# Key and probability transposes of a latent attention moved from TensorE to DMA, and five joins moved to GpSimd

## The reference, cut to what matters

```python
q = (_rmsnorm(q_lat, q_norm_g) @ wq_b).reshape(b, s, MLA_HEADS, MLA_NOPE + MLA_ROPE)
kv = (_rmsnorm(kv_lat, kv_norm_g) @ wkv_b).reshape(b, s, MLA_HEADS, MLA_NOPE + MLA_V)
k_nope, v = kv[..., :MLA_NOPE], kv[..., MLA_NOPE:]
k = jnp.concatenate([k_nope, jnp.broadcast_to(k_pe[:, :, None, :], (b, s, MLA_HEADS, MLA_ROPE))], axis=-1)
q = _rmsnorm(q, qn_g)
k = _rmsnorm(k, kn_g)
...
    sc = jnp.einsum('bhqd,bhkd->bhqk', q_blk, k).astype(jnp.float32) * scale
    p = jax.nn.softmax(sc, axis=-1)
    return jnp.einsum('bhqk,bhkd->bhqd', p, v)
...
return jax.nn.silu(gate) * o
```

## Time and profile before

| what | value |
|---|---|
| time, median of 3 runs (lowest, highest) | 787.43 us (787.29, 787.88) |
| the profiled execution: its time, its span | 787.68 us, 785.9 us |
| PE busy | 778.7 us, 99% of the span |
| DVE, ACT, POOL busy | 558.9, 414.9, 31.6 us |
| DMA | 163.02 MB, mean 207 GB/s |
| time from the issue of a 512 KB load to its landing | median 4.3 us |

### The profile page before, as it was taken

The page is one execution under the profiler, slowest core; times in us unless marked ns, Lnnn a source line. Parts: engine busy times, 40 slices in busy tenths (PEclk is TensorE's granted clock), DMA queues, the critical chain, the costliest instruction groups (busy, mean ns, idle before and its releaser), DMA issues.

```text
span 785.9 us, 9964 instructions
## 1 busy us (share of the span) xinstructions
PE 778.7 (99%) x3852; PEld 659.2 (84%) x3852; DVE 558.9 (71%) x712; ACT 414.9 (53%) x579; POOL 31.6 (4%) x36
## 2 busy tenths in 40 slices
PE   8999999999999999999999999999999999999998
PEld 7988878888888888888889888788888888888887
DVE  5873599678576756767896727997785697566684
ACT  7686756545444634533564676565555364454331
POOL 0111110000000000000000201100000000000000
PEclk9999999999999999999999999999999999999999
DMA  8895774686564837868867857765684648478875
GB/s 294 274 329 189 255 227 158 167 216 211 186 180 141 243 108 213 237 185 251 233 194 238 272 173 237 206 197 169 171 252 149 188 148 237 128 196 244 202 233 165
DMA packets 97086, 163.02 MB, mean 207 GB/s; under 512 B 57856, under 2 KB 60416, under 8 KB 96912
## 3 DMA queue, kind: packets, MB, share of 16 engines
q1 hardware_dynamic: 96432, 159.93, 68.5%
q10 hardware_dynamic: 432, 1.22, 0.5%
q0 software_dynamic: 176, 1.25, 0.4%
HBM read 147.17 MB, written 2.10 MB: 190 GB/s over the span
## 4 chain that ended last, share of the span: by engine, by line
PE 85%; DVE 10%; ACT 2%; issue 1%; POOL 1%; DMA 1%; SPq 0%; ACTq 0%
PE pair L525 56%; PE bank L484 14%; PE pair L484 6%; DVE lo L1097 4%; PE bank L452 1%; ACT work L989 1%; PE bank L445 1%; PE bank L567 1%; PE bank L768 1%; PE bank L662 1%; PE bank L758 1%; DVE yT L1349 1%; ACT hi L805 1%; POOL work L1652 1%; DMA raw<-stream 1%
## 5 line engine op out<-in xcount | busy, mean ns | idle before, releaser
L1097 DVE TENSOR_TENSOR lo<-raw,hi 128x1024 fp32r<-128x1024 f32 (+3 forms) x264 | 307.0, 1176 | 127.3 <-ACT hi L805 125.2
L805 ACT ACTIVATE hi<-raw 128x1024 fp32r<-128x1024 f32 (+3 forms) x264 | 264.1, 1021 | 208.5 <-PE pair L525 77.8
L525 PE MATMUL pair<-hi,xT_hi 128*128 128x512 f32 (+1 forms) x768 | 205.8, 388 | 2.3 <-ACT hi L805 1.2
L525 PE MATMUL pair<-lo,xT_hi 128*128 128x512 f32 (+1 forms) x768 | 202.6, 384 | 0.7 <-DVE lo L1097 0.7
L525 PE MATMUL pair<-hi,xT_lo 128*128 128x512 f32 (+1 forms) x768 | 202.7, 384 | 0.0
L525 PEld LDWEIGHTS pair<-lo,xT_hi 128*128 128x128 f32 x768 | 142.7, 188 | 29.0 <-DVE lo L1097 1.5
L525 PEld LDWEIGHTS pair<-hi,xT_lo 128*128 128x128 f32 x768 | 142.9, 188 | 28.1
L525 PEld LDWEIGHTS pair<-hi,xT_hi 128*128 128x128 f32 x768 | 140.3, 188 | 30.1 <-issue 2.0
L484 PE MATMUL bank<-hi,yT 128*128 128x512 f32 x320 | 79.0, 389 | 0.0
L484 PEld LDWEIGHTS bank<-hi,yT 128*128 128x128 f32 x320 | 60.1, 188 | 12.5
L484 PE MATMUL bank<-lo,yT 128*128 128x512 f32 x160 | 42.8, 389 | 0.0
(11 more groups left out here) (174 smaller groups left out, 638.6 us busy)
## 6 DMA issues: line engine op xcount, KB each, us to landing
raw<-stream SPq DMA_DIRECT2D x264, 512.0 KB, 4.3
raw<-stream SPq DMA_DIRECT2D x16, 256.0 KB, 5.1
xT<-x_in SPq DMA_DIRECT2D x16, 128.0 KB, 4.4
out<-xT SPq DMA_DIRECT2D x3, 512.0 KB, 7.0
consts<-consts_in POOLq DMA_DIRECT2D x1, 1152.0 KB, 8.2
mats<-mats_in ACTq DMA_DIRECT2D x2, 576.0 KB, 5.1
turned<-work SPq DMA_TRANSPOSE x34, 4.6
out<-xT SPq DMA_DIRECT2D x4, 128.0 KB, 1.7
```

What stands on the lines that cost most here:

```text
L525: return nc.tensor.matmul(pair[a][m][:, 0:width], x_part[:, slots[i], m * P:(m + 1) * P], w_part[r][:, i * 512:i * 512 + width], start=(sl ...
L805: nc.scalar.activation(cut[0], cut[1], ACT.Copy).then_inc(rounded[r].sem, 1)
L1097: nc.vector.tensor_tensor(cut[0], cut[1], cut[2].bitcast(F32), ALU.subtract).then_inc(split[r].sem, 1)
```

## The change

- **Queries.** `q` is parted and turned unscaled: DVE parts it right after it is complete, the two turns stand ahead of loads 39 and 40 instead of 44 and 45. The scale per row, with the softmax's factor, goes into the exponential (`scale=q_rs`) and the subtracted maximum.
- **Keys.** PE's 8 transposes of the keys fall away; DVE parts the scaled keys, SP turns them ahead of loads 48 and 49, DVE joins them, ACT rounds and DVE splits one tile of 128 x 1024 from SBUF.
- **Scores to probabilities.** DVE splits granules 52 and 53 before the first maximum, ACT rounds granules up to 54 before the first exponential.
- **Probabilities.** PE's 16 transposes fall away. DVE parts the probabilities of 128 tokens at a time (`p0` after granule 55, `p1` after 56), SP turns `p0` ahead of loads 57 and 58 and `p1` ahead of 61 and 62, DVE joins `p0` after granule 58 and `p1` after 62. PE multiplies the first 128 tokens with v after granule 58 and the second after 61. The turn of `u` moves from loads 55, 56 to 53, 54, that of `zb` from 64 to 66, of `D` from 68 to 70.
- **Joins.** Those of `zq`, `u`, `D`, `rq`, `B` move from DVE to GpSimd, between its reciprocal roots.
- Buffers of the work area move where the longer lives need it; on ACT the taking of `gv` comes ahead of the decays.

```diff
-TURNS = (("zq", 1), ("q", 2), ("u", 1), ("zb", 1), ("D", 1), ...
+TURNS = (("zq", 1), ("q", 2), ("k", 2), ("u", 1), ("p0", 1), ("p1", 1), ("zb", 1), ("D", 1), ...
@@ SP
+                if name in ("p0", "p1"):
+                    sp.dma_start_transpose(turned_tile[:, m], halves[:, m]).then_inc(turned.sem, 16)
...
-                    for name, at, parts in (("zq", 20, parts_q), ("q", 44, parts_h), ("u", 55, parts_h),
-                                            ("zb", 64, parts_h), ("D", 68, parts_y), ("rq", 85, parts_r),
+                    for name, at, parts in (("zq", 20, parts_q), ("q", 39, parts_h), ("k", 48, parts_h),
+                                            ("u", 53, parts_h), ("p0", 57, probs_parts[0]),
+                                            ("p1", 61, probs_parts[1]), ("zb", 66, parts_h), ("D", 70, parts_y), ...
@@ PE
-                for f in range(2):
-                    pe.wait_ge(*la_ready.at(l, f + 1))
-                    pe.wait_ge(*k_scaled.at(l, 1))
-                    turn(2 + f, [kv_sb[:, m, h, 0:NOPE] for h in (2 * f, 2 * f + 1)
-                                 for m in range(MT)]).then_inc(tk_filled.sem, 1)
...
-                turn_probs(0)
-                turn_probs(1)
-                granules(56)
+                granules(59)
+                pe.wait_ge(*probs_ready.at(l, 8))
+                pe.wait_ge(*whole_ready.at(l, TURN["p0"]))
                 times_v(0)
+                granules(62)
+                pe.wait_ge(*whole_ready.at(l, TURN["p1"]))
                 times_v(1)
-                turn_probs(2)
-                turn_probs(3)
-                granules(58)
-                times_v(2)
-                times_v(3)
@@ ACT
-                for m in range(MT):
-                    splits(53 + m)
+                act.wait_ge(*whole_ready.at(l, TURN["k"]))
+                nc.scalar.activation(yT_hi[:, SLOT["A"]:SLOT["A"] + HEADS, :], ...
+                splits(55)
+                for m in range(MT):
                     for f in range(2):
...
-                                                 ACT.Exp, bias=neg_top[:, at:at + 1], scale=QK_W ** -0.5,
+                                                 ACT.Exp, bias=neg_top[:, at:at + 1], scale=q_rs[:, at:at + 1],
@@ DVE
-                    nc.vector.tensor_tensor(q_sb[:, m], q_sb[:, m], bcast(per_head(q_rs)[:, m], 2, QK_W), ALU.mult
-                                            ).then_inc(q_scaled.sem, 1)
...
-                for m in range(MT):
-                    splits(53 + m)
+                dve.wait_ge(*q_rs_ready.at(l, 1))
+                splits(54)
+                for m in range(MT):
                     for f in range(2):
...
+                def part_probs(m):
+                    dve.wait_ge(*probs_ready.at(l, 4 * m + 4))
+                    nc.vector.tensor_copy(probs_parts[m], probs[:, m].rearrange("p h j -> p (h j)").bitcast(U16)
+                                          .rearrange("p (c a) -> p a c", a=2)).then_inc(parted.sem, 1)
+
                 splits(56)
-                dve.wait_ge(*probs_ready.at(l, 8))
+                dve.wait_ge(*whole_ready.at(l, TURN["u"]))
+                part_probs(0)
+                splits(57)
+                part_probs(1)
                 chained(nc.vector.reciprocal(p_inv, p_sum))
...
+                splits(59)
+                join(probsT[0].rearrange("p h j t -> p (h j t)"), "p0")
...
+                splits(63)
+                join(probsT[1].rearrange("p h j t -> p (h j t)"), "p1")
@@ GpSimd
+                def join(words, name):
+                    pool.wait_ge(*turned.at(l, 32 * TURN[name]))
+                    pool.tensor_copy(words.bitcast(U16).rearrange("p (t a) -> p a t", a=2),
+                                     turned16[:].rearrange("p (a k) t -> p a (k t)", a=2)
+                                     ).then_inc(whole_ready.sem, 1)
```

More of the change, by code:

```diff
@@ L645, in _, with times_v @@
                 scores_d(1)
[L646 to L659, removed]
-                    for m in range(MT):
+                def times_v(m):
+                    for h in range(HEADS):
                         for j in range(MT):
-                            mm = nc.tensor.matmul(bank[m][:, h * HD:(h + 1) * HD],
-                                                  probsT[:, h % 2, j, m * P:(m + 1) * P],
+                            mm = nc.tensor.matmul(bank[m][:, h * HD:(h + 1) * HD], probsT[m][:, h, j, :],
                                                   kv_sb[:, j, h, NOPE:NOPE + HD],
@@ L959, in _ @@
                 take("pv", lambda m: u[:, m, :], x_rs, u_ready)
[L960 removed]
+                splits(43)
                 act.wait_ge(*whole_ready.at(l, TURN["q"]))
@@ L969, in _ @@
                     nc.scalar.activation(rotary(SLOT["D"], i, i), bank_rows(0, i), ACT.Copy).then_inc(qr_rounded.sem, 1)
-                for f in range(2):
-                    act.wait_ge(*tk_filled.at(l, f + 1))
-                    nc.scalar.activation(yT_hi[:, SLOT["A"] + 2 * f:SLOT["A"] + 2 * f + 2, :],
-                                         bank[2 + f][:].rearrange("p (h t) -> p h t", h=2), ACT.Copy, scale=gains[:, G_QK + 1:G_QK + 2]
-                                         ).then_inc(kT_rounded.sem, 1)
                 splits(50)
@@ L1003, in _ @@
                 splits(61)
-                act.wait_ge(*pv_done.at(l, 4))
+                take("gv", lambda m: v_b[:, m, :], x_rs, v_b_ready)
+                splits(64)
+                act.wait_ge(*pv_done.at(l, 2))
                 decays(0)
-                splits(63)
-                act.wait_ge(*yD_ready.at(l, 8))
-                take("gv", lambda m: v_b[:, m, :], x_rs, v_b_ready)
+                splits(65)
                 decays(1)
@@ L1224, in _ @@
                 mean_square(lq_sq, lq_ms, Q_RANK, lq_ms_ready)
-                splits(20)
-                join(whole_q, "zq")
                 splits(21)
@@ L1407, in gated @@
                             in1=y[:, m, at], op0=ALU.mult, op1=ALU.mult).then_inc(ready.sem, 1)
-                for m in range(MT):
-                    gated(m, gate0, m, p_inv, yD_ready)
+                splits(61)
+                dve.wait_ge(*gate0_ready.at(l, MT))
+                dve.wait_ge(*pv_done.at(l, 1))
+                gated(0, gate0, 0, p_inv, yD_ready)
+                splits(63)
+                join(probsT[1].rearrange("p h j t -> p (h j t)"), "p1")
+                splits(64)
+                dve.wait_ge(*pv_done.at(l, 2))
+                gated(1, gate0, 1, p_inv, yD_ready)
                 part(gate0_row, yD_ready, 8, parts_y)
@@ L1436, in _ @@
                 splits(68)
+                join(whole_z, "zb")
                 edge = const("edge").rearrange("p (e g t) -> p e g t", e=2, g=4)
@@ L1503, in turn_sum @@
                                                 ).then_inc(turned.sem, 1)
-                splits(74)
-                dve.wait_ge(*k_b_ready.at(l, 2))
-                join(whole_d, "D")
                 splits(76)
@@ L1538, in _ @@
                 splits(88)
-                join(whole_r, "rq")
                 turn_sum(rk_rot, rk_turned)
@@ L1557, in _ @@
                 lo_heads(ka_rounded, kT_a_ready, 2, SLOT["C"])
-                splits(95)
-                join(whole_b, "B")
                 decay = const("decay").rearrange("p (h k i) -> p h k i", h=HEADS, k=3)
```

140 lines of the change are left out of this document (66 added, 74 removed).

## The result

The changed kernel takes **804.6 us** (median of 3 runs, 801.54 to 804.65) against 787.43: a ratio of 1.0202, 95% interval 1.0185 to 1.022. The forecast was 794.0 in a range of 785.5 to 800.0. Slower was right; the size was not, by 10.6 us. The profiled execution took 804.6 us, its span is 802.6.

A forecast was written before the change was run, and what follows sets the result against it. PE, busy 778.7 of 785.9 us, was taken to bound the kernel. Granule 62 starting 3.3 us later in each layer adds 6.6 to the profiled 787.68, 794.3; less 0.25 to the median, 794.0, range 785.5 to 800.

The forecast's parts named there:

- what bounds the kernel: PE, busy 778.7 of 785.9 us with waits of at most 0.6; a wait in its path costs its full length.
- the chain: Branch D, u's parting through exponentials to loads 57 and 62: granule 62 starts 3.3 us later a layer; 789 to 799, chance 0.60.
- Step 1: VectorE, first layer: u is parted at 135.5 instead of 136.0, bounds 134.7 and 136.3.
- Step 2: SP's queue: u's turn ahead of loads 53 and 54 puts the second load 3.3 us behind; granule 54 lands at 144.1.
- Step 4: Probabilities' turns: load 57 issued at 156.15, rounded at 161.45; p1's join at 178.95, granule 62 at 180.65, 3.3 us later.
- step 3: ACT: two roundings, eight exponentials in 3.6 us, taking gqk; granule 55 rounded at 152.5, a first PE wait of 1.7.
- At no cost: Column as scale is the same instruction; five joins on GpSimd, taken as 2.5 us each, put nothing on the path.
- The third rival: GpSimd's joins hold VectorE, u's join holding the negated maxima: 797, or 801 with a like loss beside rq's; chance 0.10.
- The same instruction: Exponentials: a column replaces the constant as scale at no cost; eight take 3.6 us.
- the second load behind the turn of p1: Load 62, behind both steps of p1's turn, lands 5.3 us after issue; second loads took 5.3 or 5.8.
- PE's granted clock should stay: PE's clock stays as it is; if it fell behind a 3.5 us wait, a granule at half would cost 2.7 more.
- The first rival: The ring hides the turns: PE meets no wait and keeps 4.0 us a layer, 779.4; chance 0.07.

The follow-up runs named there:

- kernel 9: Kernel 3 with the joins of zq, D and B on GpSimd again, those of u and rq on VectorE: 782.94 us.
- kernel 6: Kernel 3 with the turn of u early again, ahead of loads 53 and 54 as in the changed kernel: 790.61 us.
- kernel 3: The changed kernel with five joins on VectorE, turns of the probabilities ahead of loads 60 and 63, turn of u ahead of load 55: 781.01 us.
- kernel 1: The changed kernel with its five joins of zq, u, D, rq and B back on VectorE: 798.64 us.
- kernel 7: Kernel 1 with the turn of u ahead of load 55, the probabilities' turns ahead of loads 57 and 61 as in the changed kernel: 788.4 us.
- Kernel 4: The kernel before the change with the five joins on GpSimd and nothing else: 797.01 us.
- kernel 2: The changed kernel with the probabilities' turns ahead of loads 60 and 63 and their products one granule later: 796.05 us.
- kernel 5: Kernel 1 with a constant in place of the column as scale of the exponentials and of the negated maxima: 799.71 us.
- Kernel 8: Kernel 6 with 13 idle matmuls of 512 columns in PE's long wait ahead of granule 55: 788.75 us.

## Why the prediction was right and wrong, step by step

**Right: what bounds the kernel, and the chain.** A wait put into PE's path costs its length (the two waits of kernel 9, 0.97 and 0.89 us, go with 1.9 us of time), and more where the clock falls. The list of waits holds two that are longer than the 0.6 us that the prediction reads there, 1.5 and 1.1; both lie in the first 7 us and change nothing in the argument. To lay the prediction's times (on the axis of the kernel before) beside the changed trace, 1.3 us are taken off for the late start. Step 1: the turn of u, right behind its parting, stands at 135.45 against 135.5. Step 2: load 54 goes out 3.2 us behind the turn's start and lands at 144.3 against 144.1. Step 4: the turn of p0 stands at 156.0 against 154.85, and load 57 is rounded at 162.65 against 161.45, late by what they carry from step 3. Kernels 6 and 3 show that this chain hangs on u's turn, and kernels 1, 7, 6 and 3 that the turns of the probabilities have a price of their own.

**Wrong: "At no cost", the five joins.** This is the step whose mechanism failed, and it took the time out of the range: with the joins on VectorE (kernel 1) it is 798.64, inside it. The duration was well chosen, 2.5 us (2.52 measured), but I let the joins have "granules of time" and looked only at who waits for them. What matters is what they hold. The third rival had the mechanism and its price of 797 to 801, but put it at the maxima and said that "It decides from some 3 us of duration on"; it acts on the split of granule 53 and on a rotary product, at 2.5 us. Kernel 4 gives 9.4 us for the joins alone; kernel 1 gives 6.0 in the presence of the chain, and kernels 2 and 6 give 5.4 with the probabilities' turns late. The Trainium skill (SBUF — State Buffer, "Who interferes with whom") was right in both directions: 3.50 us for the held split, 3.51 for the held copy. The estimate from the Trainium skill (GPSIMD Engine Reference, "3.1 Elementwise"), 1.8 us for a join, by which the rival cost nothing, was too low against 2.52; the measured row decides.

**Mis-sized: the exponentials in step 3.** "The same instruction" with a column as scale takes 0.56 us, not 0.48. The row for it was at hand only in the kernel after, where eight take 4.34 us against my 3.6:

```profile
147.97 0.56 ACT L974 ACTIVATE work<-bank,work 128x256 f32<-128x256 f32 x1
...
152.31 1.29 ACT L809 ACTIVATE work<-pair,stat 128x512 f32<-128x512 f32 x2
153.85 2.01 ACT L791 ACTIVATE hi<-raw 128x1024 fp32r<-128x1024 f32 x2 [0.25 <-ACT work L809]
```

The Trainium skill (ScalarE: Activation LUTs, "What ACT_TABLE_LOAD costs") gives about 93 ns for each operand that is a column. The rows of kernel 5 agree, 0.09, and I had not looked it up. Granule 55 is rounded at 153.6 against 152.5, 1.1 us late, of which this is 0.7, and so is every step of the chain behind it.

**Mis-sized: the second load behind the turn of p1.** I took 5.3 us, from two pairs; load 62, issued at 172.73, is rounded from 178.91 on, 6.2 us later. In the changed kernel the second loads behind a turn land after anything from 3.8 to 6.7 us, so the term was less sure than its upper bound of 5.8 says; what it depends on no run shows. Together with the 1.1 this makes up 2.0 of the 2.35 us by which granule 62 starts later than step 4 says (183.0 against 180.65).

```profile
169.55 1.23 SPq L393 DMA_TRANSPOSE turned<-sums_all  x1
170.83 0.58 SPq L422 DMA_DIRECT2D raw<-stream  x1
171.45 1.23 SPq L393 DMA_TRANSPOSE turned<-sums_all  x1
172.73 4.89 SPq L422 DMA_DIRECT2D raw<-stream  x4
```

```profile
178.91 1.06 ACT L791 ACTIVATE hi<-raw 128x1024 fp32r<-128x1024 f32 x1 [2.90 <-DMA raw<-stream]
```

**Wrong: "PE's granted clock should stay".** It fell to half behind waits in both layers. The price named, 2.7 us for a granule at half, is the right size; 1.6 us were lost in the first layer and 2.8 in the second. In the changed kernel a later wait follows, on a chain that does not run through PE, so most of it can't have reached the end; that is argued from the trace. Kernel 8 shows what it costs where less is waiting behind: 1.9 us in two layers.

**The sum.** For both layers: the chain 6.6 forecast, 12.7 measured in the profile; the joins' 2.7 beside `rq` and `D`; the start's 1.3. Of the chain's 6.1 us too many, the rounding of granule 55 and load 62 place some 4.4 and u's join, which held the maxima in the second layer, 0.6; the rest is open. So in the traces what the chain lost beyond its forecast weighs more (5.5 us without u's join) than the joins (3.3). What stays open as well is what the joins cost within the changed kernel: the two traces of it and of kernel 1 give 3.3 us once the start is taken out, the medians 6.0.

The first rival (the ring hides the turns, 779.4) did not come, but its condition can be made: put the turns where the ring can absorb them and the time is 781.0.

## What to carry to other kernels

A load that stood behind a waiting turn went out only behind it (load 57 at 158.61, its turn at 157.33); so look in the queue for the first load that stands behind an instruction waiting for a long chain, and move the wait behind as many loads as the ring holds. Moving work to an idle engine is not free when the two engines hold each other off: ask which instructions of the other engine start while it runs, and cut it into pieces that are shorter than they are. Waits in series can cover one another, so price a cause beside the others that stay: the five joins cost 9.4, 6.0 or 5.4 us here, the join of `D` 0.3 in the changed kernel's trace and 3.0 in kernel 2's. It need not be so: the two places of the turns cost nearly the same with and without each other.

## What the runs showed of the hardware

- A copy of 128 x 2048 uint16 words on GpSimd takes 2.52 us. A split of 1.22 us on VectorE that starts 0.03 us behind it takes 3.50; started the other way round, 0.1 us behind a split, GpSimd's copy takes 3.51. With the copy in four pieces the split takes 1.76.
- An exponential of 128 x 256 with a column as scale follows the one before after 0.545 us, with a constant after 0.45.
- PE ran at a granted clock of 0.50 (1.2 GHz) at once or from at most 1.5 us behind waits of 2.06 to 3.85 us, though not behind every one (2.46, 2.47, 2.54 and 3.19 us had full clock behind them). Thirteen idle matmuls in such a wait kept it at 1.00.
- In branch D of the changed kernel's first layer the second 512 KB load behind a pair of DMA transposes landed after 5.6 (granule 54), 5.4 (58) and 6.2 us (62); in the second layer after 4.9, 3.8 and 6.6. The median of all its loads is 4.4.
